# Expert weights in 4 MB units of 32 KB rows instead of 2 MB chunks of 16 KB rows

## What is computed

```
def moe_ffn(h, w_router, b_router, w_up, b_up, w_down, b_down):
    logits = h @ w_router + b_router
    top_vals, top_idx = lax.top_k(logits, 4)
    gates = softmax(top_vals)
    # for each expert e and the tokens xb that chose it:
    u = xb @ w_up[e] + b_up[e]                    # 1024 -> 2048
    glu = minimum(u[:, 0::2], 7.0)
    lin = clip(u[:, 1::2], -7.0, 7.0)
    a = glu * sigmoid(1.702 * glu) * (lin + 1)    # 1024
    y += gate * (a @ w_down[e] + b_down[e])       # 1024 -> 1024
```

## Time and profile before

| | |
|---|---|
| median of 3 runs | 1195.04 us |
| lowest and highest | 1192.61 and 1196.85 us |
| the profiled execution | 1195.48 us, its span 1193.7 us |
| PE busy | 1140.9 us, 96% of the span |
| DVE busy | 375.6 us, 31% |
| ACT busy | 160.7 us, 13% |
| DMA | 441.95 MB, mean 370 GB/s |

### The profile page before, as it was taken

One profiled execution on the slowest core, in us unless ns is written; L12 is line 12 of the kernel. 1 busy time (PEld: TensorE's weight loads), 2 busy tenths in 40 slices (PEclk: granted clock), 3 DMA queues, 4 the chain that ended last, 5 costly groups with the idle time before them and its releaser, 6 DMA issues.

```text
span 1193.7 us, 13706 instructions
## 1 busy us (share of the span) xinstructions
PE 1140.9 (96%) x5396; PEld 506.0 (42%) x5396; DVE 375.6 (31%) x757; ACT 160.7 (13%) x296; POOL 16.6 (1%) x31
## 2 busy tenths in 40 slices
PE   8999999999999999999999999999999999999997
PEld 5688888653333333333333232323232323232322
DVE  3655263654223222222231212222222222131312
ACT  2122314421101010101000010101010101010101
POOL 2000001000000000000000000000000000000000
PEclk9999999999999999999999999999999999999999
DMA  9944335738999999999999999999999999999995
GB/s 302 377 163 143 110 136 183 310 130 319 425 407 428 428 427 428 429 429 429 427 430 428 428 428 429 428 429 429 429 428 428 429 428 428 429 429 429 428 428 239
DMA packets 49865, 441.95 MB, mean 370 GB/s; under 512 B 4618, under 2 KB 10858, under 8 KB 25020
## 3 DMA queue, kind: packets, MB, share of 16 engines
q1 hardware_dynamic: 47512, 434.72, 87.7%
q0 software_dynamic: 1648, 5.83, 1.6%
q10 hardware_dynamic: 676, 1.00, 0.3%
HBM read 440.23 MB, written 2.36 MB: 371 GB/s over the span
## 4 chain that ended last, share of the span: by engine, by line
PE 70%; DMA 28%; ACT 1%; DVE 0%; issue 0%; SPq 0%; DVEq 0%
PE pB L1214 35%; DMA ring<-in_w_up 25%; PE pA L1214 21%; PE pM L1214 9%; DMA ring<-in_w_down 3%; PE pM L1217 2%; PE pA L1217 2%; DMA x<-in_x_prompt 0%; ACT area L728 0%; DVE area L784 0%; ACT hn L604 0%; ACT hn L615 0%; DVE hn L774 0%; DVE keys L1180 0%; ACT area L723 0%
## 5 line engine op out<-in xcount | busy, mean ns | idle before, releaser
L1214 PE MATMUL pA<-ring,hn 128*64 128x512 f32 x1520 | 342.4, 594 | 20.4 <-DMA ring<-in_w_up 20.4
L1214 PEld LDWEIGHTS pA<-ring,hn 128*64 128x64 f32 x1520 | 105.4, 137 | 241.2 <-issue 201.7
L1214 PE MATMUL pB<-area,ring 128*128 128x264 f32 (+1 forms) x928 | 185.7, 390 | 0.1
L1214 PE MATMUL pB<-ring,area 128*64 128x512 f32 (+1 forms) x800 | 175.3, 595 | 1.7 <-DMA ring<-in_w_down 0.9
L1214 PEld LDWEIGHTS pB<-area,ring 128*128 128x128 f32 (+1 forms) x928 | 145.0, 177 | 34.1 <-issue 3.1
L1144 DVE TENSOR_SCALAR area<-pA 128x512 f32<-128x512 f32 x32 | 22.1, 691 | 388.7 <-PE pA L1214 388.6
L1214 PE MATMUL pA<-area,hn 128*64 128x512 f32 x528 | 119.2, 594 | 7.5 <-DMA area<-in_w_up 7.5
L1214 PEld LDWEIGHTS pB<-ring,area 128*64 128x64 f32 (+1 forms) x800 | 53.8, 135 | 101.6 <-issue 97.9
L1214 PE MATMUL pM<-area 128*128 128x512 f32 (+1 forms) x192 | 77.2, 608 | 12.4 <-ACT area L728 12.4
L1214 PE MATMUL pB<-area 128*64 128x512 f32 (+2 forms) x344 | 76.3, 547 | 1.9 <-DVE area L758 1.2
L1214 PEld LDWEIGHTS pA<-area,hn 128*64 128x64 f32 x528 | 36.9, 137 | 83.4 <-issue 67.2
(11 more groups left out here) (240 smaller groups left out, 679.6 us busy)
## 6 DMA issues: line engine op xcount, KB each, us to landing
ring<-in_w_up SPq DMA_DIRECT2D x95, 2048.0 KB, 32.1
ring<-in_w_down SPq DMA_DIRECT2D x47, 2048.0 KB, 29.3
area<-in_w_up SPq DMA_DIRECT2D x33, 2048.0 KB, 32.4
area<-in_w_down SPq DMA_DIRECT2D x16, 2048.0 KB, 30.6
ring<-in_w_in SPq DMA_DIRECT2D x24, 1024.0 KB, 10.7
ring<-in_w_out SPq DMA_DIRECT2D x4, 1024.0 KB, 6.5
area<-rev_scratch POOLq DMA_DIRECT2D x4, 512.0 KB, 6.8
ring<-in_w_down SPq DMA_DIRECT2D x2, 1024.0 KB, 32.2
```

Source lines behind the costliest of these rows:

```text
L1214: return pe.matmul(out, w, m, start=start, stop=stop, skip_group_check=True)
```

## The change

**Units.** The eight places become four units of 8192 floats a partition: ring slots 0 and 1, 2 and 3, 4 and 5, and one stretch of `area` (`unit`). A unit is filled by one DMA of 4 MB with rows of 32 KB: four rows of w_up or eight rows of w_down a partition. A pair has six units. `ring_free` rises when the second half of a unit is used, and SP waits for the unit four turns back. In the last pair each unit comes as two DMAs of 2 MB with rows of 16 KB, and PE waits for each half; so does the first unit of pair 1.

**Columns.** A partition of w_down's unit now holds eight consecutive rows, where a chunk held four. So that the turn of `act_out` still meets the right rows, the two halves `a` of up take alternate groups of eight columns instead of 1024 in a row (`columns_of`); the bias does too. The features of the tokens follow the new order of w_up's rows: `x_turn` steps by four instead of two, the first gather takes pairs of columns (`piece`), and ffn_norm_w is loaded in the same order.

**The first pair.** It still has chunks of 2 MB with rows of 16 KB, ten of them ahead. The single-use places now take chunks 2 and 7 (the third and the eighth), and the other eight go to their half units. The slots of w_in and w_out are shifted by three (`place`), so that half units come free in order.

**Other tiles.** `gpick` now lies over the router's weights, which are dead by then; `glu`, `lin`, `sig`, `act_out`, `gateT` change places within `area`.

The diff, cut to its core:

```diff
+UP_CHUNKS, DOWN_CHUNKS = 4, 2
+SINGLE = {2: 1, 7: 0}
+FIRST_PLACE = {0: 0, 1: 1, 3: 2, 4: 3, 5: 4, 6: 5, 8: 6, 9: 7, 10: 0, 11: 1}
+FIRST_ORDER = [0, 7, 1, 3, 2, 4, 9, 5, 6, 8, 10, 11]
+FREED = {j: FIRST_CHUNKS + n + 1 for n, j in enumerate(FIRST_PLACE)}
+UNIT = [1, 2, 3, 0]
+def place(c):
+    return (c + 3) % SLOTS
...
+        def unit(u):
+            if u < SLOTS // 2:
+                return ring[:, 2 * u:2 * u + 2, :].rearrange("p a n -> p (a n)")
+            return area[:, at[0]:at[0] + 2 * SLOT]
...
-            up = w_up.rearrange("(i e) (j p r) n -> e j i p (r n)", e=2, p=128, r=UP_ROWS)
-            down = w_down.rearrange("(i e) (j p r) n -> e j i p (r n)", e=2, p=128, r=DOWN_ROWS)
+            up = w_up.rearrange("(i e) (q p r) n -> e q i p (r n)", e=2, p=128, r=ROWS)
+            down = w_down.rearrange("(i e) (p r) n -> e i p (r n)", e=2, p=128)
...
+            def whole(b, i, turn):
+                u = UNIT[turn % UNITS_KEPT]
+                sp.dma_start(unit(u), rows_of(b, i)).then_inc(unit_full[u], 16)
+            def half(b, i, turn, h):
+                u = UNIT[turn % UNITS_KEPT]
+                f = slice(SLOT * h, SLOT * h + SLOT)
+                sp.dma_start(unit(u)[:, f], rows_of(b, i)[:, f]).then_inc((unit_half, unit_full)[h][u], 16)
...
+            for h in range(2):
+                sp.wait_ge(ring_free, FREED[3 + h])
+                half(0, 1, 0, h)
+            for b in range(1, PAIR_CHUNKS):
+                sp.wait_ge(ring_free, FREED[(0, 6, 9, 11)[b]] if b < UNITS_KEPT else LOOP_FREED + b - UNITS_KEPT + 1)
+                whole(b, 1, b)
...
+                    def columns_of(w, a, n):
+                        g = w.rearrange("p (g a c) -> p g a c", a=2, c=2 * ROWS)
+                        return g[:, 64 * n:64 * n + 64, a]
...
-                                o = 2048 * (k % UP_ROWS) + 1024 * a + 512 * n
-                                mm = matmul(out(a, n), xsT[:, k, 64 * e:64 * e + 64], w[:, o:o + 512],
+                                row = w[:, 2048 * (k % 2):2048 * (k % 2) + 2048]
+                                mm = matmul(out(a, n), xsT[:, k, 64 * e:64 * e + 64], columns_of(row, a, n),
                                             start=(k == 0), stop=(k == KT - 1 and n == 0))
```

More of the change, by code:

```diff
@@ L286, in build @@
         bias_up = keys.bitcast(BF16)
[L287 to L293, removed]
+        BASE = 2 * KT * NT - SLOT
+        at = [BASE + n * SLOT for n in range(4)]
+        single = [area[:, at[2]:at[2] + SLOT], area[:, at[3]:at[3] + SLOT]]
+        raw_up = area[:, at[3]:at[3] + 2 * FF]
+        raw_down = area[:, at[3] + 2 * FF:at[3] + 3 * FF]
+        two = Area(at[2])
+        aT = two.take(1024).rearrange("p (e r s) -> p e r s", e=2, r=ROWS)
         y_pair = two.take(D)
+        gateT = two.take(NT)
+        two.at = at[3]
         glu = two.take(FF).rearrange("p (e f) -> p e f", e=2)
@@ L297, in build @@
         sig = two.take(FF).rearrange("p (e f) -> p e f", e=2)
-        gateT = two.take(NT)
-        gpick = two.take(3 * 128).rearrange("p (m e s) -> p m e s", m=3, e=2)
-        two.at = places[3] + SLOT
+        act_out = two.take(FF).rearrange("p (e f) -> p e f", e=2)
+        assert two.at == at[3] + SLOT
         bias_down = two.take(D // 2).bitcast(BF16)
@@ L513, in _, with rows_of @@
[L513 to L516 removed]
+                    sp.dma_start(dst, src).then_inc(ring_full[place(c)], 16)
+            up = w_up.rearrange("(i e) (q p r) n -> e q i p (r n)", e=2, p=128, r=ROWS)
+            down = w_down.rearrange("(i e) (p r) n -> e i p (r n)", e=2, p=128)
+            def rows_of(b, i):
+                src = up[b // 2, b % 2, bass.ds(i, 1)] if b < UP_CHUNKS else down[b - UP_CHUNKS, bass.ds(i, 1)]
+                return src.rearrange("a p n -> (a p) n")
@@ new lines, in whole, with pair @@
+            def whole(b, i, turn):
[5 more added lines that the diff above has]
+                sp.dma_start(unit(u)[:, f], rows_of(b, i)[:, f]).then_inc((unit_half, unit_full)[h][u], 16)
+            def pair(pairs2, odd, i):
+                for b in range(PAIR_CHUNKS):
+                    turn = (ODD if odd else EVEN) + b
+                    sp.wait_ge(ring_free, 2 * PAIR_CHUNKS * pairs2 + (LOOP_FREED + turn - UNITS_KEPT + 1))
+                    whole(b, i, turn)
@@ new lines, in _ @@
+            for h in range(2):
[4 more added lines that the diff above has]
+                whole(b, 1, b)
+            with sp.Fori(1, PAIRS // 2 - 1) as h:
+                pair(h, 0, h * 2)
+                pair(h, 1, h * 2 + 1)
+            pair(PAIRS // 2 - 1, 0, PAIRS - 2)
+            for b in range(PAIR_CHUNKS):
+                turn = 2 * PAIR_CHUNKS * (PAIRS // 2 - 1) + ODD + b
+                sp.wait_ge(ring_free, LOOP_FREED + turn - UNITS_KEPT + 1)
+                for h in range(2):
+                    half(b, PAIRS - 1, turn, h)
```

194 lines of the change are left out of this document (87 added, 107 removed).

## The result

| | before | after |
|---|---|---|
| median | 1195.09 us (16 runs) | 1198.10 us (16 runs) |
| lowest and highest | 1192.61 and 1198.01 us | 1195.55 and 1200.23 us |
| the profiled execution | 1195.48 us, its span 1193.7 us | 1197.36 us, its span 1195.4 us |
| from PE's first up matmul to the end of its last matmul | 915.1 us | 912.8 us |

The change makes the kernel 3.0 us slower: the ratio is 1.0026, 95% interval 1.0017 to 1.0036. The last line of the table already says where to look. The stage of the expert pairs became 2.3 us shorter; what made the kernel slower happened ahead of it.

What follows compares the result with a forecast made beforehand. Transfers were taken to bound the kernel once their queue stays full, PE having a little room. From the profiled 1195.48 us, +3.8 (hand-over) - 5.7 (rows) + 1.0 (end) gave 1194.6 us; range 1188.5 to 1201.5.

Steps and rivals of the forecast that it cites:

- The rest: Small edits, mostly before the pairs: taken as 0, gather at most 2 us, bias splits delayed a microsecond or two harmlessly.
- Rival D: Main stage: longer idle stretches bring PE's clock down; 1197 to 1200 us, slower or the same; chance 0.06.
- The rows of 32 KB: Loads of whole units, pairs 1 to 14: fewer per-row constants, 0.70% less time, -5.7 us.
- The gaps in the hand-over: Pair 0 to pair 1: freeing 4 MB at once leaves the transfer queue empty 11.3 us instead of 7.5, +3.8 us.
- All five issues: SP's queue in the hand-over: loads issued near 288.8, 292.9, 300.0, 315.7 and 337.6 us.
- from issue to first data: Hand-over: a load issued into an empty queue takes 1.7 us until its data begins.
- The end: Last pair: the last 2 MB come whole instead of cut in two, so PE waits, +1.0 us.
- Groups of eight: Up matmuls of each pair: moving operand read in groups of eight floats with gaps, taken to cost zero.
- Rival B: Up matmuls: the operand in groups of eight streams slower; at 48%, PE is the bound, about 1375 us; chance 0.12.
- The sum of the stretch: Expert pairs: hand-over +3.8, rows -5.7 and end +1.0 us together.
- A: Unit loads: rows of 32 KB save nothing, or are split into 16 KB packets; 1200.3 us, slower; chance 0.16.
- C: Unit loads: the larger rows lose the whole per-row constant, -11.4 us; 1188.9 us, faster; chance 0.12.

Runs made afterwards that it cites:

- e2_before_early: The kernel before, with chunk 2's load issued ahead of chunk 1, nothing else: 1202.35 us, ratio to before 1.0062.
- e1_order: The changed kernel with chunk 7's load issued behind chunks 1 and 3 instead of ahead of chunk 1: 1193.50 us, ratio to before 0.9989.
- e3_rows16: e1_order with every 4 MB unit loaded as two DMAs of 2 MB with rows of 16 KB: 1199.59 us, ratio to before 1.0038.
- experiment 4: The run of e3_rows16 against e1_order, number of loads and of rows doubled together: 1199.59 us, 6.1 us above e1_order.
- e8_all: e5_best with chunk 7's load directly behind chunk 1 instead of behind chunks 1 and 3: 1191.56 us, ratio to before 0.9970.
- r1_order: The kernel of e1_order run again, on one chip with three others: 1192.76 us, ratio to before 0.9976.
- r4_halves1: e1_order with the first four units of pair 1 loaded as halves, run again on one chip with three others: 1192.97 us, ratio to before 0.9976.
- e5_best: e1_order with pair 1's first four units as halves and the last 2 MB as two 1 MB loads: 1193.42 us, ratio to before 0.9982.
- e7_wait: The changed kernel, its order kept, with SP waiting for all six bias loads before issuing chunk 7: 1192.65 us, ratio to before 0.9985.

## Why the prediction was wrong, point by point

**The step that failed** is in "The rest": chunk 7, issued beside the bias rows, "may delay the bias splits by a microsecond or two, and only chunk 2's load waits for these". Three things in it are wrong.
- The size. The rows came 9 us later (median), not one or two. SP's loads and POOL's loads were moved together at 279 to 322 GB/s (windows of 4 us from 196 to 212), and the six bias loads and both 2 MB loads were all done only when nearly all of their 5.4 MB had passed. The trace of after counts each queue's packets, q1 being SP's and q0 POOL's (packets, MB, share of the engines' time); here from 200 to 213 us:

```profile
q1 hardware_dynamic: 210, 3.08, 75.4%
q0 software_dynamic: 210, 0.99, 23.9%
```

  From 206 to 212 us the same view has 94 packets of each. One packet of POOL's goes for each one of SP's, while their bytes stand one to three. POOL's queue has 288 packets here, 192 rows and 96 ends, 18 for each engine. An estimate: 18 turns behind a 16 KB row of 611.9 ns each are 11.0 us; the last of POOL's loads landed after 16.1 us in place of 5.2, the median 14.2 in place of 4.9, and in e2_before_early 15.6. The Trainium skill, DMA: Bandwidth & Descriptors, "Queues, rings and completion order", says that an engine takes the queues it has work for in turn, a packet each, and puts a packet at some 9 to 17 descriptors. The trace agrees with the turns and not with their size: a turn here is one row or one end.
- Who waits. I looked for the waits on the split's semaphore and found SP's only. But ACT itself waits for the rows, in order, with the sigmoid tiles of the input projection behind the split, and PE waits for these. The prediction asked that question of the queues of SP and not of ACT.
- What comes after. PE's stop of 2.94 us brought 1.8 us more at half clock. Rival D had this mechanism, but I looked for it in the main stage, where PE has room, and not here, where it has none.

**The rows of 32 KB: right.** -5.7 us forecast, 6.0 (stretches) and 6.1 (medians) measured between e1_order and e3_rows16. A constant for each row, taken from two lengths and carried to a third, gave the size; that it belongs to the row and not to the load is not shown (experiment 4).

**The gaps in the hand-over: right, a little less.** All five issues came where they were put, behind the common delay. Measured over the 78 us from the issue of chunk 10 on, before moves 378 GB/s and after 363; against 428.4 and 431.5 (the full rates of before and after in the main stage) that is 9.2 and 12.4 us lost, +3.3 where +3.8 was forecast. One reading under it was loose: the 1.7 us "from issue to first data" are time lost and not a late start. Behind the issue at 292.96 rows already start 1.0 us later, but slowly: 246 GB/s from 293.9 to 295.1 us, 314 in the next 1.2 us, then 437.

**The end: right.** +1.0 forecast; the wait is 0.88 us, and the cut took off 1.2.

**Groups of eight: right.** 28.50 us for 136 matmuls in both. Rival B's price was read too quickly, though. It took 209 against 141 ns for the step of two floats, but weight loads of the input projection, which are as large and have no step, take 192 ns in before:

```profile
L1214 PEld LDWEIGHTS pB<-area,ring 128*128 128x128 f32 x672 | 127.2, 192 | 23.8 <-issue 2.2
```

So not all of the 48% need be the step's; no run here separates it.

The sum of the stretch was -0.9 us and came out as -2.3. With the measured terms, +3.3 - 6.0 + 1.2, it would be -1.5; the other 0.8 us are not accounted for (a step of 1 GB/s in the rate over 78 us is 0.2 us of it). With the delay, the measured -2.3 + 4.6 = +2.3 us; the two profiled executions differ by 1.9 and the medians by 3.0. The rest is in what comes behind PE's last matmul (4.3 us in after, 4.9 in before) and in the scatter of single executions.

**The rivals.** A (no gain from the rows) and C (the whole constant) fell with the rate of 431; e3_rows16 is A built on purpose, and its 1199.6 us lies near the 1200.3 worked out for it. B fell with the pair of 55.14 us. D: a stretch at half clock does occur in the main stage of after, and it costs nothing there:

```profile
1045.17 8.78 PE L1235 MATMUL pA<-ring,hn 128*64 128x512 f32 x32 [2.40 <-DMA ring<-in_w_up]
```

32 matmuls take 8.78 us instead of 7.1. In the chain of waits, the pairs that end a DMA wait at 986.87, 1045.17 and 1103.45 are 58.3 and 58.3 us apart all the same: the loss fits into the next wait.

The range of 1188.5 to 1201.5 held the time; the sign it leaned to was wrong, and none of the rivals was the one that came. That the time lies inside owes something to luck: the range was made wide for the rows and the gather, and a delay of 4.6 us that stands in no term happened to fit.

## What to carry to other kernels

When a load is moved ahead of others, price the small loads that it now shares the engines with by their packets, and not by their bytes; then ask which engine waits for them and what stands behind that wait in its queue, until the question reaches the engine that sets the end. A stop of PE in a stage where it has no room costs more than its length, since the clock may be down behind it. And where run-to-run scatter is as large as the effect, compare a stretch of the trace that leaves the scattering part out: here it separated edits of 1 us that the medians of ten runs had put in the wrong order.

## What was not expected of the hardware

**The scatter of the runs has a place.** The first 32 matmuls of the input projection, behind a stop of 1.5 us, take 7.36 us in e8_all and 9.04 in r1_order:

```profile
14.39 7.36 PE L1243 MATMUL pB<-area,ring 128*128 128x264 f32 x32
```
```profile
14.54 9.04 PE L1235 MATMUL pB<-area,ring 128*128 128x264 f32 x32
```

In r4_halves1 it is 9.88. The granted clock is 1.00 from 14 to 22 us in e8_all, and 0.50 from 16 to 18 in r1_order. The same code with the same stop got the lower clock for a different time in each execution, or not at all, and all that follows is shifted by it: the first up matmul of kernels without the collision stands between 271.96 (e8_all) and 276.25 us (e5_best). That is as wide as the 4 us over which the runs of one kernel are spread; that it accounts for the unprofiled runs too is only inferred.

**Small rows among large ones are dear.** With SP's 16 KB rows and POOL's bias rows in flight the engines were busy (shares of 0.99 to 1.02 in the windows from 200 to 212 us) and moved 295 to 322 GB/s, where SP's rows alone move 428. Most of this is the own price of the bias rows, which are 8 and 4 KB long. In e7_wait they go alone, at 223 GB/s with the engines as busy:

```profile
200.00:202.00 2.00, 2.00 (x11) 1.71 (x10) 0.00 (x0) 0.00 (x0) 0.00 (x0) 1.00 1.01 223
```

An estimate: the 3.08 and 0.99 MB that went from 200 to 213 us would take 7.2 us at 428 GB/s and 4.4 at 223, 11.6 in all where it took 13. Only the last 1.4 us would be the cost of mixing them.
